# Hidden blocks summed once before they are stored, their loads moved to SyncE's line, and a reordered start of the first layer

## The reference

```
def rmsnorm(x, w):
    xf = x.astype(jnp.float32)
    y = xf * lax.rsqrt(jnp.mean(xf * xf, axis=-1, keepdims=True) + EPS)
    return (y * w.astype(jnp.float32)).astype(x.dtype)

def swiglu(h, w_gate, w_up, w_down):
    return (jax.nn.silu(h @ w_gate) * (h @ w_up)) @ w_down
...
    x = x + (0.5 * swiglu(rmsnorm(x, p['norm_ffn1']), p['w1_gate'], p['w1_up'], p['w1_down'])).astype(x.dtype)
    y, new_state = token_mix(rmsnorm(x, p['norm_mix']), p, past)
    x = x + y.astype(x.dtype)
    x = x + (0.5 * swiglu(rmsnorm(x, p['norm_ffn2']), p['w2_gate'], p['w2_up'], p['w2_down'])).astype(x.dtype)
```

## Time and profile before

| | |
|---|---|
| time, three runs | median 2301.75 us (2301.37 to 2306.05) |
| the profiled execution | 2299.27 us, its span from first to last instruction 2297.5 us |
| PE matmuls | busy 2112.5 us, 92% of the span |
| DVE / ACT / POOL | busy 1242.8 / 780.5 / 319.1 us |
| mean granted TensorE clock | 0.962 of 2.4 GHz |

### The profile page before, as it was taken

How to read it: one execution, slowest core, us unless ns; L and a number is a source line. 1 busy time by engine, 2 the same in 40 slices (tenths; PEclk the granted TensorE clock), 3 DMA queues, 4 the chain that set the end, 5 groups by cost and what they waited for, 6 DMA issues and landing times.

```text
span 2297.5 us, 36074 instructions
## 1 busy us (share of the span) xinstructions
PE 2112.5 (92%) x15227; PEld 2022.1 (88%) x15227; DVE 1242.8 (54%) x1750; ACT 780.5 (34%) x1223; POOL 319.1 (14%) x423
## 2 busy tenths in 40 slices
...
DMA packets 58752, 270.05 MB, mean 118 GB/s; under 512 B 6568, under 2 KB 11016, under 8 KB 49248
## 3 DMA queue, kind: packets, MB, share of 16 engines
...
## 4 chain that ended last, share of the span: by engine, by line
PE 69%; DVE 12%; DMA 11%; issue 4%; POOL 3%; ACT 1%; SPq 0%; ACTq 0%; POOLq 0%; DVEq 0%
PE ps L165 61%; DMA sb_h_raw<-h_kept 10%; DVE sb_down_lo L738 2%; DVE sb_h_lo L807 2%; POOL sb_h_raw L761 2%; PE ps L1144 2%; PE ps L1183 2%; DVE sb_h_raw L780 2%; PE ps L1156 1%; DVE sb_nrm L272 1%; PE ps L209 1%; POOL sb_rms L185 1%; DVE sb_x L384 1%; DMA sb_h_first_raw<-h_kept 1%; DVE sb_seg L1828 1%
## 5 line engine op out<-in xcount | busy, mean ns | idle before, releaser
L165 PE MATMUL ps<-sb_xh,sb_up_hi 128*128 128x272 f32 x2480 | 720.2, 290 | 32.0 <-ACT sb_t L530 17.0
L165 PE MATMUL ps<-sb_xl,sb_up_hi 128*128 128x272 f32 x2480 | 719.7, 290 | 0.0
L165 PE MATMUL ps<-sb_xh,sb_up_lo 128*128 128x272 f32 x2480 | 719.2, 290 | 0.0
L165 PEld LDWEIGHTS ps<-sb_xh,sb_up_hi 128*128 128x128 f32 x2480 | 472.1, 190 | 38.6 <-issue 26.7
L165 PEld LDWEIGHTS ps<-sb_xh,sb_up_lo 128*128 128x128 f32 x2480 | 471.7, 190 | 0.0
L165 PEld LDWEIGHTS ps<-sb_xl,sb_up_hi 128*128 128x128 f32 x2480 | 471.5, 190 | 0.0
L165 PE MATMUL ps<-sb_h_hi,sb_down_hi 128*128 128x272 f32 x1188 | 359.4, 302 | 95.3 <-DVE sb_down_lo L738 95.3
L165 PE MATMUL ps<-sb_h_hi,sb_down_lo 128*128 128x272 f32 x1188 | 355.8, 299 | 0.0
L165 PE MATMUL ps<-sb_h_lo,sb_down_hi 128*128 128x272 f32 x1188 | 355.7, 299 | 0.0
L165 PEld LDWEIGHTS ps<-sb_h_hi,sb_down_hi 128*128 128x128 f32 x1188 | 237.7, 200 | 101.4 <-DVE sb_down_lo L738 101.4
L165 PE MATMUL ps<-sb_nh,sb_whi 128*128 128x362 f32 (+1 forms) x696 | 233.0, 335 | 6.4 <-ACT sb_fq L991 4.4
...
## 6 DMA issues: line engine op xcount, KB each, us to landing
sb_down_raw<-wb SPq DMA_DIRECT2D x92, 704.0 KB, 5.1
...
```

Of the source, the lines that this page charges most:

```text
L165: mm = K.nc.tensor.matmul(out, a, b, start=first and n == 0, stop=last and n == 2, skip_group_check=loose)
```

## The change

1. **h is stored by its sums.** h_kept becomes (7, 128, 11, 544): one plane for each pass. Over a pair of column tiles (2j, 2j + 1) there are four blocks of h; two planes are plain blocks, five are sums, which DVE makes in the up stage after P4 of every odd c (`h_sums`, H_SUMS), and POOL stores. Pair j = 10, the last, is summed behind the first pass's chunks. The down weights' rows are reordered on the host to fit. In the down stage a chunk is one load with 4352 contiguous bytes per partition; `chunk_sum` is gone. The last chunk of pass 0 is read from SBUF.
2. **SP's line carries all loads of the down stage.** `down_sp` issues the h chunks between the weight loads, in an order fixed by when their buffers come free. The chunks have three staging buffers instead of two, weight terms five single slots instead of two double ones. POOL only stores h and reloads x.
3. **DVE's order in a down step** is: updates, weight lo of g + 1, h lo, weight sum of g + 2. The updates of groups 0 to 4 are put off (UPDATED_AT).
4. **Last column tile:** weight hi of group 0 moves from P2 to P5, and the first chunks move by one product.
5. **Start:** ones and vector constants are loaded ahead of x. DVE squares the second quarter; for the third and fourth POOL adds ACT's eight squares, so that PE has one matmul each. `up_first_pe` takes both m for each k. T3 and T4 are summed and split after P1 and P2 of c = 1 instead of before them, and T2's and T1's order in the start changes.
6. The reload of x for the output projection is issued by SP instead of POOL, on a semaphore used before for x's quarters.

```
 DOWN = (
-    (((1, 1, 0), (1, 1, 1)), ((1, 0, 0),), ((1, 1, 0), (-1, 1, 1))),
-    (((1, 1, 0), (-1, 0, 0)), ((1, 0, 0), (1, 0, 1)), ((1, 1, 1),)),
+    (((1, 1, 0), (1, 1, 1)), 0, ((1, 1, 0), (-1, 1, 1))),
+    (((1, 1, 0), (-1, 0, 0)), 5, ((1, 1, 1),)),
...
+def first_sum_pool(K, e, N):
+
+    for c in (2, 3):
+        for k in range(1, KT):
+            n = (KT - 1) * (c - 2) + k
+            e.wait_ge(N.f.sq, N.was.sq + KT * (c - 1) + k + 1)
+            if k > 1:
+                e.wait_ge(N.f.added, N.was.added + n - 1)
+            K.nc.gpsimd.tensor_tensor(first_square(K, c, 0), first_square(K, c, 0), first_square(K, c, k),
+                                      ALU.add).then_inc(N.f.added, 1)
...
 def up_first_pe(K, e, N, rstds, between=None):
-    for n, (m, tau, bank) in enumerate(((0, 0, 4), (1, 0, 6), (0, 1, 2), (1, 1, 0))):
...
+    for tau in range(2):
...
+        for k in range(KT):
+            e.wait_ge(N.f.xlo, N.was.xlo + KT * tau + k + 1)
+            for m in range(2):
...
         elif q == P4:
             gated(K, e, N, c, 0)
             gated(K, e, N, c, 1)
+            if c % 2 and c < FT - 1:
+                h_sums(K, e, N, c // 2)
...
+        if c == 1 and q == P1:
+            xsum_lo(K, e, N, X_T3, 0)
+            xsum_lo(K, e, N, X_T3, 1)
+            xsum_dve(K, e, N, X_T4, 0)
+            xsum_dve(K, e, N, X_T4, 1)
+        if c == 1 and q == P2:
+            xsum_lo(K, e, N, X_T4, 0)
+            xsum_lo(K, e, N, X_T4, 1)
         if c == FT - 1:
...
-            for ch in {P5: (0, 1), P7: (2,), P3: (3,), P4: (4, 5)}.get(q, ()):
+            for ch in {P5: (0,), P7: (1, 2), P3: (3,), P4: (4, 5)}.get(q, ()):
                 chunk_lo(K, e, N, ch)
+            if q == P4:
+                down_sum(K, e, N, 1)
+                h_sums(K, e, N, KF - 1)
...
+def h_sums(K, e, N, j):
...
+    for q, (a, b, op) in enumerate(H_SUMS):
+        K.nc.vector.tensor_tensor(h_stage(K, j, q), h_block(K, j, *a), h_block(K, j, *b), op)\
+            .then_inc(N.f.hsum, 1)
...
+def down_sp(K, e, N, wd, hs):
...
+    for m, (g, t) in enumerate(TERMS):
+        if m >= RAWS:
+            while chunk < NP * NCH and chunk_freed(chunk) < TERMS[m - RAWS][0] - 0.7:
+                load_chunk(chunk)
+                chunk += 1
+        if m == 0:
+            e.wait_ge(N.f.alo, N.was.alo + PRODUCTS)
+        elif m == 2:
+            e.wait_ge(N.f.prod, N.was.prod + PRODUCTS)
+        elif m >= RAWS:
+            e.wait_ge(N.f.blo, N.was.blo + TERMS[m - RAWS][0] + 1)
+        load(g, t, N.f.bw[m % RAWS])
...
+UPDATED_AT = [()] * 3 + [(0,), (1, 2), (3, 4)] + [(g - 1,) for g in range(6, GROUPS)]
 def down_dve(K, e, N, last=None):
...
-        if g:
-            down_update(K, e, N, g - 1)
-        if g + 1 < GROUPS:
-            down_sum(K, e, N, g + 1)
...
+        for u in UPDATED_AT[g]:
+            down_update(K, e, N, u)
         if g + 1 < GROUPS:
             down_lo(K, e, N, g + 1)
-        for n in chunks:
-            chunk_lo(K, e, N, n)
+        if p + 1 < NP:
+            for ch in CHUNKS_AT[d]:
+                chunk_lo(K, e, N, NCH * (p + 1) + ch)
+        if g + 2 < GROUPS:
+            down_sum(K, e, N, g + 2)
```

More of the change, by code:

```diff
@@ L294, in product_at @@
     return (1 + (n - FIRST) // 7, (n - FIRST) % 7)
-def loads_of(values):
-    return sum(16 * v for v in values)
 def up_weight(K, n):
@@ L560, in gated @@
         e.wait_ge(N.f.hst[c % 2], N.was.hst[c % 2] + 16 * (c // 2))
+        e.wait_ge(N.f.hsum, N.was.hsum + 5 * (c // 2))
     cols = slice(HALF * tau, HALF * tau + HALF)
@@ L664, in up_pool @@
+    for j in range(KF - 1):
+        store(j)
+    store(KF - 1)
     e.wait_ge(N.f.hclo, N.was.hclo + NCH)
+    e.wait_ge(N.f.hss, N.was.hss + 32 * KF)
+    e.wait_ge(N.f.hst[0], N.was.hst[0] + 16 * KF)
+    e.wait_ge(N.f.hst[1], N.was.hst[1] + 16 * KF)
     e.dma_start(K.x[:, 4:8], x_src[:, 4:8]).then_inc(N.f.xl[1], 16)
```

358 lines of the change are left out of this document (189 added, 169 removed), and 10 rows, old and new, of the table DOWN.

## The result

The changed kernel takes 2154.08 us (median of four runs, 2153.6 to 2156.53), 148 us less than the kernel before (2302.36, with one run more than when the prediction was written). The ratio is 0.9355, with a 95% interval of 0.9339 to 0.9372. The profiled execution took 2153.6 us, its span 2151.8, so 145.7 less than that of before.

The account below looks back on a forecast made before the run. In the down stages PE waits for DVE's weight split, late behind h sums and double loads. 2299.27 - 59.6 - 65.5 (down stages) - 7.6 - 3 (beginnings) = 2163.6, forecast 2164 us, range 2148 to 2190.

Parts of the forecast that it names:

- Head of the down stage: Start of each down stage: group 1 starts 18 us after the end of the up stage.
- 27 groups of 8.30 us: Rest of each down stage: the 27 groups after the head take 8.30 us each, without waits.
- Stalls from x and the stored sums: Pass 1 chunks share DMA engines with x's reload and stored h sums: 4 us per layer, bounds 0 to 10.4.
- First beginning: Start of the first layer: earlier constants, POOL additions and later T3 and T4 work give -7.6 us.
- Second, -3: Start of the second layer: T3 and T4 work moved behind the first products gives -3 us (0 to 6).
- The reload of x for the output projection: Moved to SP ahead of one weight load; same semaphore wait as before and slack, so 0 us.
- Moving the issue from POOL to SP is itself worth nothing: Down-stage h loads: POOL was late only through waiting for L807, and SP waits for the same split.
- DVE is over the line even without waits: Old down stage: DVE's work in a two-chunk step is 9.5 us against 8.3 for a group.
- the third rival: Down stage: three h buffers refilling only after each split become a serial ring; 2374 us at 22 us landings; chance 0.03.
- the first (SP's line holds h back): Down stage: chunks wait behind weight loads that wait for a split; 2205 us if a third stays; chance 0.12.
- The second (POOL blocks DVE wholly): First layer's start: POOL's 14 additions add 10.8 us, so the beginning gives 2 instead of 7.6; 2169 us; chance 0.11.
- fourth rivals: Down-stage passes: something else, such as the update, held PE; only the beginnings gain, 2289 us; chance 0.02.

Follow-up runs that it names:

- e_updates: The changed kernel with every down-stage update right after its group, as before the change; 2177.5 us.
- e_pool: The changed kernel with POOL instead of SP issuing the h chunks of passes 1 to 6, behind its last stores and one half's x reload; 2190.7 us.
- e_pool_ahead: As e_pool, but the first three chunks of pass 1 are issued ahead of POOL's stores of the last sums and ahead of x; 2188.0 us.
- e_sums: The changed kernel with 60 additional DVE operations in the down stages, sized and placed like the removed h sums, ahead of the weight split; 2170.4 us.
- e_stages2: The changed kernel with two staging buffers for h instead of three, each chunk still one load; 2165.5 us.

## Why the prediction came out as it did

The time lay 10 us below the forecast and inside the range. The terms of the sum, one by one:

- **Head of the down stage, 18 us predicted, 14.9 measured in both layers.** That is to the end of group 1's weight split; PE itself begins group 1 after 15.3 and 15.9 us, behind its rest of group 0. The order of the chain was right, the landings were too long: I took 4.8 to 5.5 us for the third and fifth chunk from the earlier trace rows. In the changed kernel ACT's casts show 3.7 us for both: the low part of the first chunk ends at 507.5, that of the third at 513.6, and

```profile
511.21 1.10 ACT L879 CAST sb_h_hi<-sb_h_first_raw 128x1088 fp32r<-128x1088 f32 x1 [4.40 <-DMA sb_h_first_raw<-h_kept]
517.37 1.10 ACT L879 CAST sb_h_hi<-sb_h_first_raw 128x1088 fp32r<-128x1088 f32 x1 [1.14 <-issue]
```

  Both kernels make one load for each of these chunks. The loads now have 4352 contiguous bytes for each partition and go out from SP instead of POOL; which of it made them shorter no run separates.

- **27 groups of 8.30 us: right.** From group 8 to the end all groups take that, in both layers.
- **Stalls from x and the stored sums, 4 us predicted (0 to 10.4): 1.9 and 3.2** (counted from PE's own start of group 1: 1.5 and 2.2). The collision is there (422 GB/s between 543.3 and 560.0), and a load of x that took 10.7 us to land takes 19.6, but the deferred updates cover it; e_updates prices that cover at 12 us a layer. What is left is one wait of PE for a weight split in each layer: 1.25 us at 544.9, where the fourth chunk (issued at 527.91) came to ACT's cast only 9.9 us later, for the most part while the last sums were stored and not yet beside x (issued at 535.83), and 1.73 us at 1957.5, behind chunks that landed late beside x. With the head this is 9.1 of the 10 us.

```profile
543.30:560.00 16.70, 15.45 (x123) 15.23 (x123) 14.06 (x14) 5.83 (x6) 0.00 (x0) 1.00 1.02 422
```

- **First beginning, -7.6 predicted: -7.2. Second, -3: -3.2.** The second half of the items began at 40.21 (40 predicted) by the path that was argued: the items end at 35.77 (35.7), PE's products two us later. P7 follows the stall at 79.90, two products further than P6 before, which stood at

```profile
80.50 0.56 PE L165 MATMUL ps<-sb_xh,sb_up_hi 128*128 128x272 f32 x1 [8.48 <-ACT sb_t L530]
```

  From there to the copy of the last P5 the 140 products take 422.8 us, 3.02 each, so the sums of h cost nothing, as predicted. The second layer's 478.6 us are 477.4 to 478.6 in the nine other kernels whose start is the same, so its gain is 3.2 to 4.3.
- **The reload of x for the output projection: 0 predicted.** The mixer is 1.0 us shorter; in the changed kernel and its twelve variants this stretch takes 664.8 to 669.6 us, so that is scatter.

Two steps of the argument were wrong, though no term of the sum hung on them. **"Moving the issue from POOL to SP is itself worth nothing"** failed: e_pool and e_pool_ahead show some 17 us a layer. It holds for the chunks from pass 2 on; ahead of those of pass 1 POOL's line had, in pass 0, the stores of the last sums, the wait for them and 4.4 MB of x. I had listed what waits on POOL's line, but not asked what a chunk stands behind there once h is stored by its sums. **"DVE is over the line even without waits"** (9.5 us against 8.3) explained nothing: e_sums carries the same DVE work through passes of 33.2 us, because the one-chunk steps give back what the two-chunk steps overrun. What made the old passes long is a ring: pairs of buffers that come free only at the split, whose two loads are both needed ahead of the next step's weight split. The prediction had this mechanism, but as the third rival, against the changed kernel; it is the kernel before that it describes. The change broke it by one load for each chunk; with that two buffers already give passes of 33.2 us (e_stages2), and the third is worth 11 us, in pass 0.

Of the rivals, the first (SP's line holds h back) would show waits for h in every pass; there are 25.1 us in all, nearly all of it in the first two passes of each layer. The second (POOL blocks DVE wholly) was near: my own sign for it, items two us apart, did appear (2.4 us), but it was badly chosen, since the forecast's own 17.5 us for eight items are 2.2 each. The size decides: 6.4 us of DVE's time beside 14 additions, where 5.8 was forecast and 10.8 was the rival's. By the rule of the Trainium skill, SBUF — State Buffer, "Who interferes with whom", each addition would have locked DVE out until it finished; the trace shows less. The last addition, with DVE idle, took 0.77 us, so 14 of them would be 10.8, and 6.4 were added to DVE; the other additions took 1.06 to 1.36 us, so POOL was held up too, and its 16.8 us are not the price. The third and fourth rivals did not occur.
